# One encoder layer on one core: the first product of the feed-forward opening is moved ahead of four token blocks' transposes, and the first weights' low parts are moved to GpSimd

## The chip, the cores and the metric

One core of one Trainium2 chip runs the whole program. The metric is the device time of one execution in microseconds (us), the median of the runs shown. Engines: PE is TensorE's matmuls, PEld its weight loads, DVE is VectorE, ACT is ScalarE, POOL is GpSimd, SP is SyncE, which here only issues DMAs.

## What is computed

A prompt of 1024 tokens and a sample of 64 tokens, 1024 features each, go through one layer in float32:

```python
x = x + 0.5 * swiglu_1(rmsnorm(x, g_ffn1))   # w1_gate, w1_up: 1024 x 2816; w1_down: 2816 x 1024
x = x + mix(rmsnorm(x, g_mix))               # sliding-window attention and mLSTM heads
x = x + 0.5 * swiglu_2(rmsnorm(x, g_ffn2))
y = rmsnorm(x, g_final)
# rmsnorm(x, g) = x * rsqrt(mean(x * x) + 1e-6) * g;  swiglu(h) = (silu(h @ w_gate) * (h @ w_up)) @ w_down
```

The change lies in the opening of swiglu_1. The rest is as before, but for counts in waits that follow from it.

## The kernel before, in words

**Features on partitions.** The 1088 tokens come in nine blocks, eight of 128 and one of 64 (numbered 0 to 8). TensorE transposes each block in two halves of four tiles into PSUM banks (`start_transpose`, L836 to L846), ACT or DVE copies it from there to X (`start_evict_act`, L848; `start_evict_dve`, L853). The columns are worked on in two halves j of 544 tokens, and each of these in two pieces of 272 (n is 0 to 3 over all of them).

**Norm.** ACT squares and sums each block as it lies by tokens (`start_block_square`, L858) and takes the roots of a group of blocks (`start_block_root`, L866). DVE takes their reciprocals and writes them on diagonals (`start_diagonals`, L871). TensorE multiplies the diagonals by ones, which puts the scale of every token on all partitions in PSUM bank 4 + n (`start_roots`, L879). DVE scales a piece of X by it and by the gain (`start_scale`, L922).

**Split operands.** Every float32 operand is split in a high part, a copy to the matmul type on ACT (`start_high` L941, `start_weight_high` L957), and a low part, the difference of the two (`start_low` L948, `start_weight_low` L963, both on DVE). `three_pass` (L289) does three matmuls for one product of two split tiles.

**The first pair.** FFN columns come in pairs of 128. The first pair is multiplied out in 16 chains of 24 matmuls (`start_chain`, L967): four for the gate weights and four for the up weights (mat 0 and 1) in each half j. Chains of j 0 are worked on in pieces th of 272 tokens and column blocks fh. Chain i adds up in bank i. `start_silu` (L993, ACT) empties the gate banks, `start_gate` (L997, DVE) multiplies the up banks in. Later pairs use seven products instead of eight (`pe_stage`), which need differences of X's pieces: `start_difference` (L1004, DVE), `start_third_high` (L1024, ACT) and `start_third_low` (L1037, DVE) make them.

**X is scaled in place in the half j 1.** So SyncE first stores X to memory, in four DMAs xsp<-X (`spill`, L457 to L465): two for j 0, then two for j 1, which wait for ten copies by ACT (`x_evA`), that is for the last block. `start_scale` of j 1 waits for these stores (`x_out`, L932). SyncE's queue holds behind them the loads of the second pair's weights (RAWG, RAWU).

**Order.** Each engine's order is written out by hand: `start_pe_tokens` and `start_pe_pair` (L1045, L1053), `start_act_tokens` and `start_act_pair` (L1072, L1125), `start_dve_tokens` and `start_dve_pair` (L1136, L1191). GpSimd makes constants, issues small loads, and then has nothing to do until it adds weights for the second pair (`weight_sums`, L545 on). After the first pair `up_pe` runs the second pair's four stages (mat and j 0 or 1, seven products each). DVE empties their banks (L703), ACT copies some (L617), and both make the next weights' parts in between (L578, L583).

## Time and profile before

| | |
|---|---|
| median of 3 runs (lowest, highest) | 1945.61 us (1944.47, 1946.06) |
| the profiled execution's own time | 1945.54 us |
| its span in the profile | 1944.0 us |
| PE busy | 1924.2 us, 99% of the span |
| DVE, ACT, POOL busy | 1284.3, 783.4, 1053.3 us |
| mean granted TensorE clock | 0.998 of full speed |

Times in the rows are from the span's start. In a row of a timeline the columns are start, length, engine, line, operation, output and inputs, shapes and count. Rows of one kind that follow each other are merged, and "<-" in brackets names what ended the idle time ahead. A length can run into the next start, as the instructions of an engine overlap; the distance from start to start is what one of them takes of its engine.

### The profile page before, as it was taken

To read this page: it belongs to the slowest core of one execution; us is meant where nothing else is said; L and a number is where in the kernel's file an instruction comes from. 1 tells how busy PE (TensorE), PEld (TensorE's weight loads), DVE (VectorE), ACT (ScalarE), POOL (GpSimd) and SP (SyncE) were. 2 spreads that over 40 slices of the span, in tenths; PEclk is the share of its full clock that TensorE was granted. 3 is DMA by queue.
4 is the path that set the end of the run, shared out by engine and by line. 5 is a ranking of instruction groups with operands and counts; after the bars stand their busy time and mean duration, and the time that the engine had idled before them with its cause. 6 is when DMAs were issued, how large, how long until landed. Compare 5 with 4: busy or idle time off the path is not lost.

```text
span 1944.0 us, 39225 instructions
## 1 busy us (share of the span) xinstructions
PE 1924.2 (99%) x14627; PEld 1882.3 (97%) x14627; DVE 1284.3 (66%) x1882; ACT 783.4 (40%) x1595; POOL 1053.3 (54%) x958
## 2 busy tenths in 40 slices
PE   8999999999999999999999999999999999999998
PEld 7999999999999999999998999999999999999997
DVE  6866777666566788864445664866767667656674
ACT  6433333333443345733334542443333333344343
POOL 2277776775777641321222442237767776686770
PEclk9999999999999999999999999999999999999999
DMA  8135445334986530342332834214454444498552
GB/s 271 46 114 178 140 162 179 132 132 156 316 311 188 169 102 14 116 119 90 100 104 62 207 94 124 79 56 145 150 180 144 132 154 164 151 362 276 165 157 104
DMA packets 226846, 293.88 MB, mean 151 GB/s; under 512 B 16616, under 2 KB 158472, under 8 KB 226736
## 3 DMA queue, kind: packets, MB, share of 16 engines
q1 hardware_dynamic: 219040, 272.76, 43.8%
q0 software_dynamic: 7696, 19.63, 3.2%
q8 instruction: 71, 1.16, 0.3%
q14 instruction: 39, 0.32, 0.1%
HBM read 198.07 MB, written 94.21 MB: 150 GB/s over the span
## 4 chain that ended last, share of the span: by engine, by line
PE 96%; DVE 1%; DMA 1%; issue 1%; POOL 1%; ACT 0%; SPq 0%; ACTq 0%; POOLq 0%
PE bank L291 29%; PE bank L292 29%; PE bank L293 29%; PE bank L2583 1%; PE bank L2602 1%; PE bank L2593 1%; DMA XIN<-in_x_prompt 1%; PE bank L2514 0%; PE bank L1332 0%; PE bank L1334 0%; PE bank L1333 0%; PE bank L1328 0%; PE bank L845 0%; PE bank L2694 0%; PE bank L2692 0%
## 5 line engine op out<-in xcount | busy, mean ns | idle before, releaser
L291 PE MATMUL bank<-HA,HW 128*128 128x272 f32 x1120 | 322.7, 288 | 0.0
L292 PE MATMUL bank<-HA,HW 128*128 128x272 f32 x1120 | 322.3, 288 | 0.0
L293 PE MATMUL bank<-HA,HW 128*128 128x272 f32 x1120 | 322.1, 288 | 0.0
L1381 DVE SCALAR_TENSOR_TENSOR HW<-WRAW,HW 128x512 fp32r<-128x512 f32 x140 | 224.5, 1644 | 103.8 <-ACT HW L1376 103.3
L1387 POOL TENSOR_TENSOR HA<-ARAW,HA 128x544 fp32r<-128x544 f32 x140 | 222.6, 1607 | 101.8 <-ACT HA L1375 101.6
L291 PE MATMUL bank<-HL,WGH 128*128 128x368 f32 (+2 forms) x784 | 255.6, 326 | 0.0
L293 PE MATMUL bank<-HH,WGL 128*128 128x368 f32 (+2 forms) x784 | 246.3, 314 | 1.1 <-issue 1.1
L292 PE MATMUL bank<-HH,WGH 128*128 128x368 f32 (+2 forms) x784 | 246.2, 314 | 0.0
L292 PE MATMUL bank<-FC,WR 128*128 128x272 f32 x768 | 222.1, 289 | 0.0
L291 PE MATMUL bank<-FC,WR 128*128 128x272 f32 x768 | 220.4, 287 | 0.6 <-DVE WR L583 0.5
L293 PE MATMUL bank<-FC,WR 128*128 128x272 f32 x768 | 220.1, 287 | 0.0
L292 PEld LDWEIGHTS bank<-HA,HW 128*128 128x128 f32 x1120 | 211.1, 189 | 0.0
L293 PEld LDWEIGHTS bank<-HA,HW 128*128 128x128 f32 x1120 | 211.1, 189 | 0.0
L291 PEld LDWEIGHTS bank<-HA,HW 128*128 128x128 f32 x1120 | 210.5, 188 | 0.2 <-POOL HA L1387 0.2
L814 POOL TENSOR_TENSOR SA<-SA,PV 128x272 f32<-128x272 f32 x160 | 140.4, 898 | 101.3 <-DVE PV L703 98.1
L583 DVE TENSOR_TENSOR WR<-RAWU,WR 128x512 fp32r<-128x512 f32 x100 | 99.3, 993 | 134.3 <-ACT WR L578 134.3
L1375 ACT ACTIVATE HA<-ARAW 128x544 fp32r<-128x544 f32 x140 | 91.6, 654 | 232.3 <-PE bank L293 163.5
L629 ACT ACTIVATE SA<-SA 128x272 f32<-128x272 f32 x160 | 67.5, 431 | 265.9 <-POOL SA L768 137.0
L703 DVE TENSOR_TENSOR PV<-bank,PV 128x272 f32<-128x272 f32 x280 | 118.5, 435 | 77.6 <-POOL PV L765 38.5
L291 PEld LDWEIGHTS bank<-HL,WGH 128*128 128x128 f32 x784 | 147.3, 188 | 14.6 <-issue 12.9
L292 PEld LDWEIGHTS bank<-HH,WGH 128*128 128x128 f32 x784 | 147.5, 188 | 1.6
L293 PEld LDWEIGHTS bank<-HH,WGL 128*128 128x128 f32 x784 | 147.4, 188 | 1.0 <-issue 1.0
(384 smaller groups left out, 5670.6 us busy)
## 6 DMA issues: line engine op xcount, KB each, us to landing
asp<-SA SPq DMA_DIRECT2D x44, 544.0 KB, 3.5
RAWG<-in_w_gate SPq DMA_DIRECT2D x22, 1024.0 KB, 6.5
RAWU<-in_w_up SPq DMA_DIRECT2D x22, 1024.0 KB, 6.4
tsp<-TT SPq DMA_DIRECT2D x40, 544.0 KB, 6.6
ARAW<-tsp SPq DMA_DIRECT2D x80, 272.0 KB, 3.4
WS<-in_w_down SPq DMA_DIRECT2D x20, 1024.0 KB, 8.6
wsp<-WS SPq DMA_DIRECT2D x20, 1024.0 KB, 8.6
WRAW<-wsp SPq DMA_DIRECT2D x80, 256.0 KB, 4.3
```

Source lines behind the costliest of these rows:

```text
L291: nc.tensor.matmul(bank[:, 0:w], w_hi, rhs_lo, start=first, stop=False)
L292: nc.tensor.matmul(bank[:, 0:w], w_hi, rhs_hi, start=False, stop=False)
L293: return nc.tensor.matmul(bank[:, 0:w], w_lo, rhs_hi, start=False, stop=last)
L583: nc.vector.tensor_tensor(WR[:, o, 1], weight(o, q0, mat), WR[:, o, 0].bitcast(F32), ALU.subtract).then_inc(s_.lo, 1)
L629: nc.scalar.activation(tile, tile, ACT.Silu).then_inc(s_.silu, 1)
L703: nc.vector.tensor_tensor(out, bank, add, ALU.add).then_inc(s_.ev, 1)
L814: nc.gpsimd.tensor_tensor(gated(j, slot), gated(j, slot), PV[j][:, tile], ALU.mult).then_inc(s_.mul, 1)
L1375: nc.scalar.activation(HA[f][h][:, 0], ARAW[r][:, :, :], ACT.Copy).then_inc(down_hi, 1)
L1381: nc.vector.scalar_tensor_tensor(out=HW[f][h][:, 1], in0=WRAW[r][:, :], scalar=0.5, in1=HW[f][h][:, 0].bitcast(F32), op0=ALU.mult, op1=ALU ...
L1387: nc.gpsimd.tensor_tensor(HA[f][h][:, 1], ARAW[r][:, :, :], HA[f][h][:, 0].bitcast(F32), ALU.subtract).then_inc(down_alo, 1)
L2583: mm = nc.tensor.matmul(BANK[2 + i // 2][:, (i % 2) * 256:(i % 2) * 256 + 256], QB[rows, par, 2 * g_ + hl // 2, :], KW[rows, par, 0 if g_ ...
L2593: tr = nc.tensor.transpose(BANK[4 + w][:, i * P:(i + 1) * P], SP[:, i, w * P:(w + 1) * P], IDENT[:, :])
```

## The change

- TensorE: the first chain comes after block 4's transposes, ahead of blocks 5 to 8 and of the second scale row. Blocks 5 to 8 and the rows stand between the chains that follow. The third row stands inside the fifth chain, the fourth behind it.
- The first scale group of three blocks becomes two, of blocks 0 and 1 and of block 2.
- Block 3 is copied by DVE, and the second half of block 2 by ACT. Block 5 goes to banks 6 and 7, block 6 to banks 2 and 3, block 7 to banks 6 and 7.
- The eight low parts of the first weights are made by GpSimd instead of DVE. The first chain waits for one of them, and for the second in its middle.
- The 16 chains take banks 0 to 5 in turn instead of 0 to 3.
- ACT's order: first operands ahead of weights, all four up weights' high parts ahead of the squares of blocks 5, 6 and 7 and of block 8's copy.
- The j 1 stores wait for nine copies by ACT, which is block 8's again.

The diff, without hunks that only renumber counts:

```diff
         NORM_BANK = (4, 5, 4)
+        GROUP = ((0, 2, P), (2, 3, P), (3, 5, P), (5, 8, P), (8, 9, DEC))
+        ROOTS = len(GROUP)
...
             elif j:
-                sp.wait_ge(x_evA, 10)
+                sp.wait_ge(x_evA, 9)
             else:
-                sp.wait_ge(x_evV, 8)
-                sp.wait_ge(x_evA, 4)
+                sp.wait_ge(x_evV, 9)
+                sp.wait_ge(x_evA, 1)
...
-        BLOCK_BANK = (0, 2, 4, 6, 2, 0, 6, 2, 6)
-        ON_ACT = (3, 5, 6, 7, 8)
-        ON_DVE = (0, 1, 2, 4)
+        BLOCK_BANK = (0, 2, 4, 6, 2, 6, 2, 6, 6)
...
             pe.wait_ge(block_in[b], 16)
-            if b in (4, 5, 7):
-                pe.wait_ge(x_evV, {4: 4, 5: 2, 7: 8}[b])
-            elif b in (6, 8):
-                pe.wait_ge(x_evA, {6: 4, 8: 6}[b])
+            if b in (4, 5, 6):
+                pe.wait_ge(x_evV, {4: 4, 5: 7, 6: 9}[b])
+            elif b in (7, 8):
+                pe.wait_ge(x_evA, {7: 3, 8: 7}[b])
...
-        def start_evict_act(act, b):
-            for half in range(2):
+        def start_evict_act(act, b, halves=(0, 1)):
+            for half in halves:
...
-        def start_evict_dve(dve, b):
-            for half in range(2):
+        def start_evict_dve(dve, b, halves=(0, 1)):
+            for half in halves:
...
             pe.wait_ge(st.dg, (3, 5, 7, 9)[n])
             if n == 0:
-                pe.wait_ge(x_evV, 6)
-            elif n == 2:
-                pe.wait_ge(x_evA, 10)
+                pe.wait_ge(x_evV, 5)
+            elif n == 1:
+                pe.wait_ge(x_evA, 1)
+            else:
+                pe.wait_ge(x_evA, 9)
...
-                dve.wait_ge(x_evV, 6 if n == 0 else 8)
-                wait_done(dve, x_evA, (0, 4, 6, 10)[n])
+                dve.wait_ge(x_evV, 9 if n else 5)
+                wait_done(dve, x_evA, (kh, 1, 5, 9)[n])
...
+        def start_weight_low_pool(pool, i):
+            pool.wait_ge(st.whi, i + 1)
+            nc.gpsimd.tensor_tensor(WR[:, i, 1], first_weight(i), WR[:, i, 0].bitcast(F32), ALU.subtract).then_inc(st.wlo, 1)
...
+        def start_bank(f, mat, j, i):
+            return BANK[i if f else (8 * j + 4 * mat + i) % 6]
+
+        def start_bank_free(pe, mat, j, i):
+
+            q = 8 * j + 4 * mat + i
+            if q < 2:
+                pe.wait_ge(x_evV, 2)
+            elif q < 4:
+                pe.wait_ge(x_evA, 5)
+            elif q < 6:
+                pe.wait_ge(st.ht, 2 * i + 2)
+            elif q in (10, 11, 12, 13):
+                pe.wait_ge(st.mul, q - 9)
+            else:
+                pe.wait_ge(st.silu, {6: 1, 7: 2, 8: 3, 9: 4, 14: 5, 15: 6}[q])
+
         def start_chain(pe, f, mat, j, i, between=None):
             fh, th = (i // 2, i % 2) if mat and j else (i % 2, i // 2)
             if j == 0:
-                pe.wait_ge(st.wlo, 8 * f + 4 * mat + 2 * fh + 2)
-            if mat:
+                pe.wait_ge(st.wlo, 8 * f + 4 * mat + 2 * fh + (2 if f else 1))
+            if f == 0:
+                start_bank_free(pe, mat, j, i)
+            elif mat:
                 pe.wait_ge(st.silu, 8 * f + 4 * j + i + 1)
             elif j:
                 pe.wait_ge(st.mul, 8 * f + i + 1)
-            elif f:
+            else:
                 pe.wait_ge(o_add, OUT_STEPS - 4 + i + 1)
-            elif i < 2:
-                pe.wait_ge(x_evA, 2)
-            else:
-                pe.wait_ge(x_evA, 8)
             for kh in range(2):
                 e = 2 * th + kh
+                if f == 0 and j == 0 and kh:
+                    pe.wait_ge(st.wlo, 4 * mat + 2 * fh + 2)
...
-                    mm = three_pass(BANK[i], HT, WR[:, slot, 0, k], WR[:, slot, 1, k], product(PLACE[e], j, 0, k, f), product(PLACE[e], j, 1, k, f),
+                    mm = three_pass(start_bank(f, mat, j, i), HT, WR[:, slot, 0, k], WR[:, slot, 1, k], product(PLACE[e], j, 0, k, f), product(PLACE[e], j, 1, k, f),
...
-            nc.scalar.activation(gated(j, i % 2 * 2 + i // 2), BANK[i][:, 0:HT], ACT.Silu).then_inc(st.silu, 1)
+            nc.scalar.activation(gated(j, i % 2 * 2 + i // 2), start_bank(f, 0, j, i)[:, 0:HT], ACT.Silu).then_inc(st.silu, 1)
...
-            nc.vector.tensor_tensor(gated(j, slot), gated(j, slot), BANK[i][:, 0:HT], ALU.mult).then_inc(st.mul, 1)
+            nc.vector.tensor_tensor(gated(j, slot), gated(j, slot), start_bank(f, 1, j, i)[:, 0:HT], ALU.mult).then_inc(st.mul, 1)
...
         def start_pe_tokens(pe):
-            for b in range(3):
-                start_transpose(pe, b)
+            pe.wait_ge(const_ops, 7)
+            start_transpose(pe, 0)
+            start_transpose(pe, 1)
+            start_transpose(pe, 2)
             start_roots(pe, 0)
-            for b in range(3, 6):
-                start_transpose(pe, b)
-            start_roots(pe, 1)
+            start_transpose(pe, 3)
+            start_transpose(pe, 4)
 
         def start_pe_pair(pe, f):
             if f:
@@ -1058,47 +1080,51 @@
                         start_sum(pe, 3)
             else:
                 start_chain(pe, f, 0, 0, 0)
+                start_transpose(pe, 5)
+                start_roots(pe, 1)
                 start_transpose(pe, 6)
+                start_chain(pe, f, 0, 0, 1)
                 start_transpose(pe, 7)
-                start_chain(pe, f, 0, 0, 1)
+                start_chain(pe, f, 0, 0, 2)
                 start_transpose(pe, 8)
-                start_chain(pe, f, 0, 0, 2)
-                start_chain(pe, f, 0, 0, 3, between=lambda: start_roots(pe, 2))
+                start_chain(pe, f, 0, 0, 3)
+                start_chain(pe, f, 1, 0, 0, between=lambda: start_roots(pe, 2))
                 start_roots(pe, 3)
-            for mat, j in ((1, 0), (0, 1), (1, 1)):
+                for i in range(1, 4):
+                    start_chain(pe, f, 1, 0, i)
+            for mat, j in ((1, 0), (0, 1), (1, 1)) if f else ((0, 1), (1, 1)):
                 for i in range(4):
                     start_chain(pe, f, mat, j, i)
 
         def start_act_tokens(act):
-            for b in range(3):
-                start_block_square(act, b)
+            start_block_square(act, 0)
+            start_block_square(act, 1)
             start_block_root(act, 0)
+            start_block_square(act, 2)
+            start_block_root(act, 1)
+            start_evict_act(act, 2, (1,))
+            start_high(act, 0, 0, 0)
             start_weight_high(act, 0, 0)
+            start_high(act, 0, 0, 1)
             start_weight_high(act, 0, 1)
             start_block_square(act, 3)
-            start_high(act, 0, 0, 0)
             start_block_square(act, 4)
-            start_block_root(act, 1)
-            start_high(act, 0, 0, 1)
-            start_evict_act(act, 5)
-            start_evict_act(act, 3)
+            start_block_root(act, 2)
             start_weight_high(act, 0, 2)
             start_weight_high(act, 0, 3)
-            start_block_square(act, 5)
+            start_evict_act(act, 5)
             start_evict_act(act, 6)
             start_high(act, 0, 0, 2)
+            start_high(act, 0, 0, 3)
             start_evict_act(act, 7)
-            start_high(act, 0, 0, 3)
-            start_weight_high(act, 0, 4)
-            start_weight_high(act, 0, 5)
-            start_block_square(act, 6)
-            start_block_square(act, 7)
-            start_block_root(act, 2)
+            for i in range(4, 8):
+                start_weight_high(act, 0, i)
+            for b in (5, 6, 7):
+                start_block_square(act, b)
+            start_block_root(act, 3)
             start_evict_act(act, 8)
             start_block_square(act, 8)
-            start_block_root(act, 3)
-            start_weight_high(act, 0, 6)
-            start_weight_high(act, 0, 7)
+            start_block_root(act, 4)
...
         def start_dve_tokens(dve):
-            for b in range(3):
-                start_evict_dve(dve, b)
+            start_evict_dve(dve, 0)
+            start_evict_dve(dve, 1)
             start_diagonals(dve, 0)
+            start_evict_dve(dve, 2, (0,))
+            start_diagonals(dve, 1)
             start_scale(dve, 0, 0, 0, 0)
             start_scale(dve, 0, 0, 1, 0)
             start_low(dve, 0, 0, 0)
-            start_diagonals(dve, 1)
-            start_weight_low(dve, 0, 0)
-            start_weight_low(dve, 0, 1)
             start_low(dve, 0, 0, 1)
+            start_evict_dve(dve, 3)
+            start_diagonals(dve, 2)
             start_evict_dve(dve, 4)
-            start_weight_low(dve, 0, 2)
-            start_weight_low(dve, 0, 3)
             start_scale(dve, 0, 0, 0, 1)
             start_scale(dve, 0, 0, 1, 1)
             start_low(dve, 0, 0, 2)
             start_low(dve, 0, 0, 3)
-            start_weight_low(dve, 0, 4)
-            start_weight_low(dve, 0, 5)
-            start_diagonals(dve, 2)
             start_diagonals(dve, 3)
+            start_diagonals(dve, 4)
...
-            start_weight_low(dve, 0, 6)
-            start_weight_low(dve, 0, 7)
...
+            for i in range(8):
+                start_weight_low_pool(pool, i)
             up_pool(pool, 0)
             down_pool(pool, 0)
```

## Rows read from the trace of the kernel before

**Rows 1.** The page: busy time of each engine, share and instructions:

```profile
PE 1924.2 (99%) x14627; PEld 1882.3 (97%) x14627; DVE 1284.3 (66%) x1882; ACT 783.4 (40%) x1595; POOL 1053.3 (54%) x958
```

**Rows 2.** What TensorE waited for in the whole span: total, times, longest (us):

```profile
PE bank L888 <- DVE DG L877: 1.7, 1, 1.7
...
PE bank L291 <- DVE WR L583: 0.5, 1, 0.5
```

**Rows 3.** Timeline of PE, 5 to 37 us:

```profile
14.61 5.38 PE L845 MATMUL bank<-IDENT,XIN 128*128 128x128 f32 x24 [1.65 <-DMA XIN<-in_x_prompt]
...
20.73 0.36 PE L291 MATMUL bank<-FC,WR 128*128 128x272 f32 x1
...
23.80 1.91 PE L845 MATMUL bank<-IDENT,XIN 128*128 128x128 f32 x16
25.47 0.37 PE L291 MATMUL bank<-FC,WR 128*128 128x272 f32 x1
...
36.95 0.38 PE L291 MATMUL bank<-FC,WR 128*128 128x272 f32 x1
```

**Rows 4.** By windows: PE, PEld, DVE, ACT, POOL busy, granted clock, DMA share, GB/s:

```profile
13.00:14.00 1.00, 0.00 (x0) 0.00 (x0) 0.93 (x3) 0.51 (x1) 0.00 (x0) 0.54 1.00 353
...
19.00:20.00 1.00, 1.00 (x7) 1.00 (x6) 1.00 (x3) 0.70 (x2) 0.00 (x0) 0.55 1.06 195
```

**Rows 5.** Timeline of ACT, 13 to 37 us:

```profile
13.49 1.15 ACT L961 ACTIVATE WR<-RAWG 128x512 fp32r<-128x512 f32 x2 [3.06 <-DMA RAWG<-in_w_gate]
...
15.64 1.10 ACT L946 ACTIVATE FC<-HJ 128x1088 fp32r<-128x1088 f32 x1
...
22.52 1.07 ACT L862 ACTIVATE JK<-XIN 128x1024 f32<-128x1024 f32 x1
...
26.41 1.09 ACT L851 ACTIVATE X<-bank 128x512 f32<-128x512 f32 x2
...
28.37 1.17 ACT L961 ACTIVATE WR<-RAWU 128x512 fp32r<-128x512 f32 x2
...
30.67 1.06 ACT L862 ACTIVATE JK<-XIN 128x1024 f32<-128x1024 f32 x1
...
31.85 0.30 ACT L869 ACTIVATE RMB<-SSB,GQOE 128x3 f32<-128x3 f32 x1
32.05 0.64 ACT L851 ACTIVATE X<-bank 128x256 f32<-128x256 f32 x2
...
36.40 1.27 ACT L995 ACTIVATE SA<-bank 128x272 f32<-128x272 f32 x4
```

**Rows 6.** Timeline of SP, the first j 1 store:

```profile
32.72 0.36 SPq L465 DMA_DIRECT2D xsp<-X  x1
```

**Rows 7.** Timeline of DVE, 16 to 99 us:

```profile
16.77 1.29 DVE L950 TENSOR_TENSOR FC<-HJ,FC 128x1088 fp32r<-128x1088 f32 x1 [0.34 <-ACT FC L946]
...
37.27 1.72 DVE L935 SCALAR_TENSOR_TENSOR X<-X,GC,bank 128x272 f32<-128x272 f32 x4 [1.37 <-DMA xsp<-X]
40.95 1.72 DVE L935 SCALAR_TENSOR_TENSOR X<-X,GC,bank 128x272 f32<-128x272 f32 x4 [1.96 <-DMA xsp<-X]
...
94.59 0.69 DVE L583 TENSOR_TENSOR WR<-RAWU,WR 128x512 fp32r<-128x512 f32 x1 [1.02 <-ACT WR L578]
...
98.30 0.78 DVE L583 TENSOR_TENSOR WR<-RAWU,WR 128x512 fp32r<-128x512 f32 x1 [2.67 <-ACT WR L578]
```

**Rows 8.** The chain that ended last, 75 to 102 us: start, length, engine and line:

```profile
76.07 0.44 DVE PV L703
...
100.45 1.40 DVE WR L583
...
101.89 0.39 PE bank L291
```

**Rows 9.** Timeline of POOL, two of the second pair's additions:

```profile
45.49 1.29 POOL L556 TENSOR_TENSOR SS<-RAWG 128x512 f32<-128x512 f32 x1 [32.82 <-DMA RAWG<-in_w_gate]
...
73.18 2.24 POOL L556 TENSOR_TENSOR SS<-RAWU 128x512 f32<-128x512 f32 x1 [6.17 <-PE bank L293]
```

More of the change, by code:

```diff
@@ L271, in build @@
         down_mm, MM_FROM = x_tr, 2 * (NB + 1)
-        down_cp, CP_FROM = x_evA, 10
-        down_ev, EV_FROM = x_evV, 8
+        down_cp, CP_FROM = x_evA, 9
+        down_ev, EV_FROM = x_evV, 9
         down_hi, HI_FROM = dist_abs, 1
@@ L325, in norm_sum @@
             if n == 2:
-                pe.wait_ge(st.rs, 4 + 1)
+                pe.wait_ge(st.rs, ROOTS + 1)
             for h in range(2):
@@ L347, in norm_reciprocal @@
         def norm_reciprocal(dve, n):
-            dve.wait_ge(st.rs, 4 + n + 1)
+            dve.wait_ge(st.rs, ROOTS + n + 1)
             nc.vector.reciprocal(square_row(n), square_row(n)).then_inc(st.rc, 1)
@@ L352, in norm_scale @@
             w = NTILE[n][1]
-            dve.wait_ge(st.rc, 4 + n + 1)
+            dve.wait_ge(st.rc, ROOTS + n + 1)
             if n:
@@ L917, in start_reciprocal @@
         def start_reciprocal(dve, n):
-            dve.wait_ge(st.rs, 7 + n + 1)
+            dve.wait_ge(st.rs, ROOTS + 3 + n + 1)
             nc.vector.reciprocal(scale_row(1, n), scale_row(1, n)).then_inc(st.rc, 1)
@@ L924, in start_scale @@
             if f:
-                dve.wait_ge(st.rc, 7 + n + 1)
+                dve.wait_ge(st.rc, ROOTS + 3 + n + 1)
             else:
@@ L2138, in _ @@
                 nc.scalar.activation(FS[0:L, b % 4, 2:3], FS[0:L, b % 4, 2:3], ACT.Sqrt, bias=EPSC[0:L, 0:1], scale=1.0 / D).then_inc(st.rs, 1)
-            act.wait_ge(st.rc, 11 + NB + 1)
+            act.wait_ge(st.rc, ROOTS + 7 + NB + 1)
             act.wait_ge(fin_gain, GAIN_FROM + 1)
@@ L2480, in _ @@
                 nc.vector.tensor_tensor(f[:, 2:3], f[:, 0:1], f[:, 1:2], ALU.add).then_inc(fin_sum, 1)
-                dve.wait_ge(st.rs, 11 + b + 1)
+                dve.wait_ge(st.rs, ROOTS + 7 + b + 1)
                 nc.vector.reciprocal(f[:, 3:4], f[:, 2:3]).then_inc(st.rc, 1)
-                dve.wait_ge(st.rc, 11 + b + 1)
+                dve.wait_ge(st.rc, ROOTS + 7 + b + 1)
                 if 4 <= b < NB:
@@ L2508, in head_sums @@
                 if LAST_SUM[i] is None:
-                    pe.wait_ge(st.rs, 4 + (2 if HEAD_BANK[i] == 5 else 3))
+                    pe.wait_ge(st.rs, ROOTS + (2 if HEAD_BANK[i] == 5 else 3))
                 else:
```

2 lines of the change are left out of this document (removed).

## Prediction, made before the change was run

> **What bounds the kernel now.** I read the page first: PE is busy for 1924.2 of 1944.0 us [rows 1]. So the change can win only where TensorE stands still or runs at half clock, and it loses where it makes TensorE wait. Next what TensorE waited for [rows 2]: 1.7 us for the diagonals, before 14.61 us, and 0.5 us once for a low part of a weight. Then the timelines. In the PE timeline block 3 starts when its DMA lands, at 14.61 after 1.65 us of waiting, and from there TensorE runs on: 24 transposes, the second scale row, the first chain at 20.73 [rows 3]. The clock rows show why that start is slow: the granted clock is 0.54 of full speed over the window from 13 to 14 us and 0.55 over that from 19 to 20 [rows 4]. It fell to 1.2 GHz at about 13.1, after TensorE had waited for the diagonals and for block 3, and rose to 2.4 GHz at about 19.9, after unbroken work from 14.61. A transpose takes 5.38/24 = 0.224 us in the slow stretch and (25.47 - 23.80)/16 = 0.104 us after it [rows 3].
>
> The last view is the chain of waits, and it decides here. At 76.07 it leaves TensorE for DVE, and comes back only at 101.89, when TensorE has stood still for 0.5 us for the low part that DVE finished at 100.45 + 1.40 = 101.85 [rows 8, 2]. Between the two DVE, ACT and GpSimd answer each other, several us behind TensorE. Before 76.07 DVE's timeline is full back to 40.95; in its short pauses it only waits for ACT's copies of its own results. At 40.95 it had waited 1.96 us, and at 37.27 1.37 us, for the stores of X's second half [rows 7]. The first of these stores is issued at 32.72 and the second right behind it [rows 6], just after ACT's copy of block 8, which ends at 32.05 + 0.64 = 32.69 [rows 5]. **So two paths lead to 101.89: TensorE's own, 0.5 us short, and block 8's copy, stores, DVE.** The second sets the end of this stretch.
>
> **TensorE's part.** Same matmuls, other order. Up to 14.61 the path is the DMA of block 3, which nothing here moves: SyncE's loads are as before, and the wait for the constants only moves into a function. From 14.61 TensorE was never idle until 20.6 and must not be in the new kernel. Blocks 3 and 4 take 16 x 0.224 = 3.6 us, to 18.2. The first chain can start then if its inputs are there. Before, the operand's first low part ended at 16.77 + 1.29 = 18.06, though ACT's copy for it had stood behind two weight copies and a square, from 13.49 to 15.64 [rows 7, 5]. Now the roots of blocks 0 and 1 are taken before block 2 is there, so only one diagonal is left behind block 2. Of TensorE's 1.7 us of waiting for the diagonals I take 1.0 as saved, and scaling starts about 1 us earlier, near 12.0. ACT copies the first operand at once, to 14.7, the first weight to about 15.3 (1.15/2 each), the second operand (1.10) to 16.3 and the second weight to 16.9. DVE's low parts of the operands (1.29 each) are done by 16.3 and 17.6, GpSimd's first two (1.29 each alone [rows 9]) by 16.6 and 18.2. So the chain starts at 18.2 instead of 20.73.
>
> That is no gain in itself. The chain costs 23.80 - 20.73 = 3.07 us at full clock [rows 3], but until 19.9 it runs at half, so its first 1.7 us do only 0.85 us of work and it ends near 22.1. Block 5 and the second scale row then follow at full clock. The same work in the same clock ends at the same time. What is won: the first chain's pause of 0.1 us for block 5's copy, and the pause ahead of the fifth chain. That one started at 36.95 because the first SiLU, which empties its bank, started at 36.40 and ended near 36.8 [rows 3, 5]; with bank 4 it doesn't wait, about 0.3 us. What is lost: two more restarts of a chain behind transposes, some 0.1 us in all. Net: TensorE 0.3 us earlier (my bounds: 0 and 0.6). Banks 0 and 1 for the seventh and eighth chains need SiLU 1 and 2, near 38.5, at 42; nothing waits there.
>
> **GpSimd's low parts.** I bound the price by 1.29 and 2.24 us, the same kind of work at 45.49 and at 73.18, where DVE was subtracting SBUF tensors beside it [rows 9]. DVE makes its two operand low parts just beside the first two. The long price puts the second at 19.8, and the chain's middle needs it at 20.5, so I cost both ends at nothing. The Trainium skill, GPSIMD Engine Reference, section Key points, says that GpSimd shares its SBUF interfaces with VectorE and contends with instructions that have two SBUF inputs. By that rule these first two go at the long price; the trace agrees (2.24 against 1.29). It leaves 0.7 us of room instead of 2.4. The six later parts lie beside scaling that reads PSUM, or beside an idle DVE. GpSimd's small loads are issued before 13 us. The six subtractions that DVE is rid of after the first two save it nothing on the path: it waits for the stores at 37.27 anyway.
>
> **ACT's part, where I see the price.** Follow ACT to block 8's copy. Before, it did block 5's square at 22.52, while it waited for TensorE. It reached the up weights at 28.37, and then did two weight copies, two squares, one root and block 8 [rows 5]. Now block 5's transposes stand behind the first chain, so ACT has nothing from about 20.5 to 22.6. TensorE: first chain to 22.1, block 5 to 22.9, scale row to 23.5, block 6 to 24.3, second chain to 27.4, block 7 to 28.2. ACT copies the second half of block 7 at 28.4 (two halves took 1.09 at 26.41) and reaches the up weights at 28.9, 0.5 us later than before. Then four weight copies instead of two, + 1.1 us (1.17 for two), and three squares instead of two, + 1.2 us (31.85 - 30.67 = 1.18). Root and copy are the same. Block 8's copy ends at 32.7 + 0.5 + 1.1 + 1.2 = 35.5, **2.8 us later**. Both stores of j 1 and the weight loads behind them in SyncE's queue go 2.8 us later, with nothing else in the DMA queues in either case. GpSimd's additions to those weights and ACT's copies of them are used only when the first pair ends, after 60 us, which covers them.
>
> DVE then gets the stores at about 40.1 and 43.8, and all that follows is 2.8 us later, up to the low part that TensorE waited for at 101.85, now 104.65. TensorE waits longer there, in all 0.5 + 0.3 + 2.8 = 3.6 us over four products, and from 101.89 + 2.8 on it runs as before. The chains of j 1 still get their inputs in time: the ninth chain at 48.5 needs an operand at about 46.7, and its middle one at 48.3 for 50.0. The second pair's third product may pause some tenths for a gate near 75, inside the 3.6 us.
>
> **Sum.** 1945.54 us of the profiled execution (span 1944.0) + 2.8 = 1948.3. The median 1945.61 is 0.07 us off that execution, which changes nothing. Bounds of the term: 1.8, a third less, if DVE's pauses or the turns between engines swallow some of it, and 3.6, if the slower GpSimd and a late second weight part hold the first chain by 0.9 us.
>
> **Rivals.**
> 1. *The DVE path has slack* that the chain of waits doesn't show, or the stores are made up for (they land faster behind an empty queue). Then only TensorE's order counts: 0.3 us earlier, and at best the 0.5 us wait gone: 1944.8 to 1945.4. Against it: two waits of DVE for these very stores [rows 7]. For it: "the chain" names the last releaser only, and at 76.07 TensorE and DVE were ready within 0.1 us of each other.
> 2. *Slower by more: TensorE's longer wait costs the clock.* Before, it waited once, 0.5 us. Now four products of one stage wait. The low parts of the fourth and fifth came at 95.3 and 99.1 [rows 7], and will at 98.1 and 101.9; TensorE wants the fifth 1.5 us after the fourth (half a chain, 3.07/2), at 99.6. It stands still for 2.3 us of 3.8, and again 1.2 us before the sixth. At 13.1 the clock fell after two pauses of 1.7 and 1.65 us around the few matmuls of the first scale row, and stayed low for 6.8 us [rows 2 to 4]. If it falls for half of that time or all of it, half of 3.4 to 6.8 us is lost: 1950.0 to 1951.7. The Trainium skill, TensorE: Matmul & The Clock Gate, section HAM oscillation, says that waits between bursts of matmuls can send the array back to the slow clock each time. By that rule this rival is likelier when the waits lump together. It makes the kernel slower by 0.2% from about 1.1 us of loss on top of my sum. A clock that rises late in the opening, because the first chain's inputs come late and break the run from 14.61, costs as much.
> 3. *The change doesn't do what it says:* the first chain starts no earlier than about 20.7, because GpSimd or ACT is late. Then block 5 and ACT's rest come 1 us or more later too, and the price is 3.7 to 4.7: about 1949.7.
>
> **The numbers.** Forecast 0.55, rival 1 0.22, rival 2 0.17, rival 3 0.04, something else faster 0.02. A measurement of this kernel can tell about 0.2% from no change, 3.9 us. The forecast and rival 1 lie within it, rival 2 nearly all outside, rival 3 half; faster by 3.9 us would need more idle time than TensorE has after 14.61. So faster 0.02, within 0.2% 0.79, slower 0.19. The range, from rival 1's better half to the near part of rival 2: 1944.8 to 1950.6.
>
> **What would show it.** Right: first chain at 18 to 18.5 with its first matmuls at about 0.25 us each; fifth chain near 35 and without a pause; block 8's copy on ACT ending at 35 to 36; j 1 stores issued right behind it; DVE waiting for them until about 40 and 43.8; TensorE waiting 3 to 4 us for WR's low parts between 93 and 105. Wrong: stores no later than at 33.5; DVE's last store wait before 42.5; TensorE's wait near 102 under 1 us; a granted clock of 0.5 after 100 us (rival 2).

## The result, and the profile after

The changed kernel takes **1951.41 us** (median of 7 runs, 1950.75 to 1953.97), the kernel before, run beside it, 1945.59 us (7 runs, 1943.76 to 1946.06). The ratio is 1.0035, with a 95% interval of 1.0026 to 1.0044: slower by 0.35%. The forecast was 1948.3, its range ended at 1950.6, and the sign that it held likeliest was no difference. The profiled execution took 1950.83 us, its span is 1949.3, which is 5.3 us more than before.

What TensorE waited for, in the whole span (total, times, longest), rows that answer to [rows 2]:

```profile
PE bank L291 <- DVE SA L1023: 4.1, 1, 4.1
...
PE bank L888 <- DVE DG L875: 1.1, 1, 1.1
```

The wait for the diagonals is 0.6 us shorter, as the change wants, but the one behind it, for block 3's data, is 0.6 us longer (2.29 instead of 1.65 us), so the saving is not kept. The wait for a weight's low part is gone. One wait of 4.1 us is new. DVE's L1023 is the gate, the multiplication that empties an up bank.

The timeline of PE, first chain, the wait, and what followed:

```profile
17.65 0.59 PE L291 MATMUL bank<-FC,WR 128*128 128x272 f32 x1
18.04 0.43 PE L292 MATMUL bank<-FC,WR 128*128 128x272 f32 x1
18.27 0.43 PE L293 MATMUL bank<-FC,WR 128*128 128x272 f32 x1
...
74.39 0.28 PE L291 MATMUL bank<-FBa,WR 128*128 128x272 f32 x1
...
80.11 0.36 PE L291 MATMUL bank<-FXa,WR 128*128 128x272 f32 x1 [4.07 <-DVE SA L1023]
...
81.28 0.43 PE L293 MATMUL bank<-FXa,WR 128*128 128x272 f32 x1
81.51 0.43 PE L291 MATMUL bank<-FXa,WR 128*128 128x272 f32 x1
...
84.45 0.30 PE L292 MATMUL bank<-FBa,WR 128*128 128x272 f32 x1
84.60 0.29 PE L293 MATMUL bank<-FBa,WR 128*128 128x272 f32 x1
84.72 0.29 PE L291 MATMUL bank<-FT,WR 128*128 128x272 f32 x1
...
107.13 0.28 PE L291 MATMUL bank<-FC,WR 128*128 128x272 f32 x1
```

The second, third and fifth product in the kernel before:

```profile
74.38 0.28 PE L291 MATMUL bank<-FBa,WR 128*128 128x272 f32 x1
...
75.87 0.28 PE L291 MATMUL bank<-FXa,WR 128*128 128x272 f32 x1
...
78.86 0.28 PE L291 MATMUL bank<-FT,WR 128*128 128x272 f32 x1
```

The first chain starts at 17.65 with its matmuls 0.23 us apart, 3.1 us earlier than before [rows 3]. At 80.11 TensorE resumes after standing still for 4.07 us; its matmuls are 0.13 us apart at first, and from about 81.1 to 84.5 they are 0.23 us apart. The products side by side give the whole account: the second starts at the same time (74.39 and 74.38), the third 4.24 us later, the fifth 5.86 us later, so that the slow stretch took 1.62. The last row is the product that waited at 101.89 before [rows 8]; here it doesn't wait and is 5.24 us later, which is the loss of the whole span but for 0.1. That the two agree so well is partly chance: what lies behind this product took 1840.8 to 1842.5 us in the profiles of all kernels here (1844.1 in experiment 8), though nothing in it was changed. So this start is a finer yardstick than the span. By windows, columns as in [rows 4]:

```profile
78.00:80.00 2.00, 0.00 (x0) 0.00 (x0) 2.00 (x3) 0.35 (x1) 0.47 (x1) 1.00 0.00 0
80.00:82.00 2.00, 1.89 (x12) 1.92 (x13) 2.00 (x4) 0.77 (x1) 0.00 (x0) 0.77 0.00 0
82.00:84.00 2.00, 2.00 (x10) 2.00 (x10) 1.97 (x4) 0.40 (x1) 0.00 (x0) 0.50 0.79 252
```

The granted clock is still whole while TensorE stands still, and falls to 1.2 GHz about a microsecond after it resumes. It stays there for some 3.4 us.

**From ACT to the wait.** ACT's four up weights and its copy of block 8, then SyncE's queue, answering to [rows 5] and [rows 6]:

```profile
28.73 2.19 ACT L961 ACTIVATE WR<-RAWU 128x512 fp32r<-128x512 f32 x4
...
34.68 0.64 ACT L851 ACTIVATE X<-bank 128x256 f32<-128x256 f32 x2
```

```profile
36.95 1.39 SPq L398 DMA_DIRECT2D RAWG<-in_w_gate  x1
38.38 1.47 SPq L398 DMA_DIRECT2D RAWU<-in_w_up  x1
```

Block 8's copy ends at 35.32 instead of 32.69, 2.63 us later. DVE's timeline after, answering to [rows 7], with the stretch ahead of the late gate:

```profile
40.09 1.72 DVE L935 SCALAR_TENSOR_TENSOR X<-X,GC,bank 128x272 f32<-128x272 f32 x4 [2.81 <-DMA xsp<-X]
44.63 1.78 DVE L935 SCALAR_TENSOR_TENSOR X<-X,GC,bank 128x272 f32<-128x272 f32 x4 [2.82 <-DMA xsp<-X]
...
47.88 2.05 DVE L950 TENSOR_TENSOR FBa<-X,FBa 128x1088 fp32r<-128x1088 f32 x1
...
73.82 2.03 DVE L1041 TENSOR_TENSOR TS<-X,TS 128x1088 f32<-128x1088 f32 x1
75.78 1.57 DVE L585 TENSOR_TENSOR WR<-RAWG,WR 128x512 fp32r<-128x512 f32 x1
77.28 2.34 DVE L1041 TENSOR_TENSOR TS<-X 128x1088 f32<-128x1088 f32 x1
79.55 0.42 DVE L1023 TENSOR_TENSOR SA<-SA,bank 128x272 f32<-128x272 f32 x1
...
105.08 1.39 DVE L585 TENSOR_TENSOR WR<-RAWU,WR 128x512 fp32r<-128x512 f32 x1 [1.02 <-ACT WR L580]
```

The same gate and what stood ahead of it, in the kernel before:

```profile
69.63 1.28 DVE L1020 TENSOR_TENSOR TS<-X,TS 128x1088 f32<-128x1088 f32 x1
70.83 0.68 DVE L583 TENSOR_TENSOR WR<-RAWG,WR 128x512 fp32r<-128x512 f32 x1
71.44 1.28 DVE L1020 TENSOR_TENSOR TS<-X 128x1088 f32<-128x1088 f32 x1
72.64 0.42 DVE L1002 TENSOR_TENSOR SA<-SA,bank 128x272 f32<-128x272 f32 x1
```

The last wait for a store ends 3.68 us later, the first of the three instructions starts 4.19 us later, the gate behind them 6.91 us later. The three take 2.03, 1.57 and 2.34 us instead of 1.28, 0.68 and 1.28: 2.7 us more. GpSimd's timeline says what lies beside them:

```profile
73.19 1.51 POOL L558 TENSOR_TENSOR SS<-RAWU 128x512 f32<-128x512 f32 x1 [1.99 <-PE bank L293]
74.78 2.02 POOL L560 TENSOR_TENSOR SS<-SS,RAWU 128x512 f32<-128x512 f32 x1
76.77 1.70 POOL L561 TENSOR_TENSOR RAWU<-RAWU 128x512 f32<-128x512 f32 x1
```

These three additions start when TensorE ends the first pair, at 73.19 after and at 73.18 before [rows 9]. They did not move, and DVE did. Before, the gate was done when they began; now DVE's three instructions lie beside them, and both engines are slowed.

### The profile page after: what moved, and what is told of

Read it like the earlier page. It is cut to its first block, busy times and chain, and to the rows that moved or that the text cites. A ratio compares the mean times of both kernels' runs of the same rounds, so it can differ in the third digit from the quotient of the medians.

```text
span 1949.3 us, 39234 instructions
## 1 busy us (share of the span) xinstructions
PE 1926.6 (99%) x14627; PEld 1884.0 (97%) x14627; DVE 1280.5 (66%) x1876; ACT 783.2 (40%) x1595; POOL 1061.4 (54%) x966
## 4 chain that ended last, share of the span: by engine, by line
PE 96%; DVE 1%; POOL 1%; DMA 1%; issue 0%; ACT 0%; SPq 0%; ACTq 0%; POOLq 0%; DVEq 0%
PE bank L291 29%; PE bank L292 29%; PE bank L293 29%; PE bank L2605 1%; PE bank L2624 1%; PE bank L2615 1%; DMA XIN<-in_x_prompt 1%; PE bank L2536 0%; PE bank L1353 0%; PE bank L1354 0%; PE bank L1355 0%; PE bank L1349 0%; PE bank L2716 0%; PE bank L2714 0%; PE bank L2706 0%
```

## The experiments

All of them ran on the chip beside the kernel before, whose median was 1944.50 us on the chip of experiments 1 to 4, 1943.79 for 5 to 8, and 1944.34 for 9 to 11. The table gives the ratio to it with its interval, and from the profiled execution the end of the low part that set 101.85 before (DVE) and the start of the product that reads it (TensorE). Where the second is later than the first by more than 0.06 us, TensorE did not wait for the low part, and its own path set the start. As the kernel before itself took 1943.8 to 1945.6 us in the four sets of runs, a band given in us is loose by that much, and the ratios are what compares.

| | ratio [95%] | low part ends | product starts |
|---|---|---|---|
| before | 1 | 101.85 | 101.89 |
| after | 1.0035 [1.0026, 1.0044] | 106.47 | 107.13 |
| 1 copy of block 8 early | 1.0003 [0.9993, 1.0012] | 101.33 | 101.39 |
| 2 before, stores late | 1.0025 [1.0015, 1.0035] | 106.96 | 107.02 |
| 3 gates first | 1.0026 [1.0017, 1.0036] | 105.80 | 105.85 |
| 4 additions behind gates | 1.0025 [1.0014, 1.0035] | 105.51 | 105.56 |
| 5 loads behind stores | 1.0039 [1.0025, 1.0052] | 106.98 | 107.64 |
| 6 both, on after | 1.0008 [0.9999, 1.0017] | 102.06 | 102.11 |
| 7 both, on before | 0.9996 [0.9987, 1.0005] | 100.91 | 100.98 |
| 8 24 added matmuls | 1.0036 [1.0025, 1.0047] | 106.88 | 106.94 |
| 9 ACT's order alone, on after | 1.0007 [0.9998, 1.0016] | 100.79 | 100.84 |
| 10 copy early, on before | 1.0001 [0.9992, 1.0010] | 101.27 | 101.36 |
| 11 32 added matmuls | 1.0033 [1.0021, 1.0045] | 106.99 | 107.04 |

**1. Block 8's copy early, all else of the change kept.**

```diff
-            for b in (5, 6, 7):
+            start_block_square(act, 5)
+            start_evict_act(act, 8)
+            for b in (6, 7):
                 start_block_square(act, b)
             start_block_root(act, 3)
-            start_evict_act(act, 8)
```

> The changed kernel, but ACT copies block 8 behind the square of block 5, ahead of those of blocks 6 and 7. Theory A (ACT copies block 8 2.6 us later, so the j 1 stores and with them DVE's whole path are late): the copy ends near 32.7 us again, the first store is issued near 32.7, DVE waits for the last store until about 41, TensorE waits for no gate near 76, its clock stays up, and the time is that of the kernel before less up to 0.8 us: 1944.8 to 1945.8. Theory B (GpSimd's weight parts and the additions beside DVE are the cause, the stores are not): TensorE still waits 3 us or more near 76, and the time stays above 1949.5. Theory C (the first chain at half clock is the cause): above 1949.5 too, with no long wait later on.

Measured: 1944.68 us, ratio 1.0003, 0.1 us under the band that I gave, on a chip whose kernel before is itself 1.1 us faster. One moved call takes back 0.32 of the 0.35%. ACT and DVE of this kernel:

```profile
31.55 0.65 ACT L851 ACTIVATE X<-bank 128x256 f32<-128x256 f32 x2
```

```profile
74.66 0.43 DVE L1023 TENSOR_TENSOR SA<-SA,bank 128x272 f32<-128x272 f32 x1
```

Block 8 is copied by 32.20, the stores go out at 32.23, and the last gate is at 74.66. TensorE has no wait between 60 and 100 us, its clock stays whole there, and only the old wait is left (0.65 us, for the low part). So the copy's place on ACT is the root of nearly all of the loss; the opening's new order, with its low parts on GpSimd, is not. It is not quite free, though: here and in experiment 3, where the clock rose about 2 us earlier in the opening, TensorE waited 0.28 and 0.25 us for GpSimd's second low part at 19.73.

**2. The other way round: before, with the stores made late.** SyncE also waits for the eight low parts of the first weights.

```diff
             elif j:
                 sp.wait_ge(x_evA, 10)
+                sp.wait_ge(st.wlo, 8)
```

> The kernel before, with one wait more: SyncE issues the two j 1 stores only when the last low part of the first weights is done, near 35.9 us instead of 32.7. Nothing of the opening's order is changed. Theory A: DVE gets the last store near 44.5 instead of 41, TensorE waits 3 to 5 us, at a gate near 76 or spread over low parts near 100, and the time is 1949 to 1952. Theories B and C: within 0.7 us of the kernel before, 1945.0 to 1946.3.

Measured: 1949.24 us, ratio 1.0025, in the band of theory A. The stores go out at 35.57, and TensorE's waits from 70 us on are

```profile
78.97 0.36 PE L291 MATMUL bank<-FXa,WR 128*128 128x272 f32 x1 [0.62 <-DVE SA L1003]
82.16 0.37 PE L291 MATMUL bank<-FBa,WR 128*128 128x272 f32 x1 [1.46 <-DVE SA L1003]
...
107.02 0.39 PE L291 MATMUL bank<-FC,WR 128*128 128x272 f32 x1 [0.72 <-DVE WR L584]
```

Late stores alone, in the old kernel, cost most of what the change costs: the product starts at 107.02, 5.1 us late. Here the waits come in more pieces with matmuls between, and the granted clock stays whole. Two of them lie in the first pair already (0.46 us at 62.33 and 0.55 at 66.13, both for SiLU, which empties one of the four banks that the old order shares), so that the second pair's second product starts at 76.70, 2.3 us late. The changed kernel, with six banks, has none of these. 2.9 us of lateness at the store's issue became 4.17 us at DVE's second wait (45.12 against 40.95).

**3. Gates ahead of the differences and low parts.** The queue behind DVE's slow instructions is reordered, in the first pair only: gates 2 and 3 follow gate 1.

```diff
             start_gate(dve, f, 1, 1)
+            if not f:
+                start_gate(dve, f, 1, 2)
+                start_gate(dve, f, 1, 3)
             start_difference(dve, f, 1, 1)
             weight_low(dve, f, 1, 0, 3, first=True)
             start_difference(dve, f, 1, 2)
-            start_gate(dve, f, 1, 2)
+            if f:
+                start_gate(dve, f, 1, 2)
...
-            start_gate(dve, f, 1, 3)
+            if f:
+                start_gate(dve, f, 1, 3)
```

> The changed kernel, but in the first FFN DVE takes the last two gates of the first pair right behind the second of that half, ahead of two differences and a weight's low part. Theory A in its full form (DVE's path up to the low parts near 105 us sets the end): the wait at the third product near 76 goes, and TensorE waits instead for low parts of weights between 94 and 106, in all 4.5 to 5.5 us: 1949.8 to 1951.0, or 1.7 more if the clock falls there. If the price was only the gate's wait and the fall of the clock behind it: below 1947.

Measured: 1949.26 us, ratio 1.0026, which is 0.5 us under the band that I gave. The gate's wait and the clock's fall are both gone. In their place TensorE waits for low parts:

```profile
80.33 0.39 PE L291 MATMUL bank<-FT,WR 128*128 128x272 f32 x1 [1.12 <-DVE WR L585]
...
103.10 0.39 PE L291 MATMUL bank<-FT,WR 128*128 128x272 f32 x1 [1.58 <-DVE WR L585]
105.85 0.39 PE L291 MATMUL bank<-FC,WR 128*128 128x272 f32 x1 [0.97 <-DVE WR L585]
```

That is 3.7 us in three waits, less than the 4.5 to 5.5 that I expected, and the first of them lies earlier. It is near the 3.6 us of the first forecast, but by luck: that one came from a DVE 2.8 us late, and here DVE is 3.95 us late (105.80 against 101.85). The lag of DVE has to be paid once, and the order of DVE's instructions chooses where.

**4. GpSimd's additions behind the gates.**

```diff
             if first and mat:
                 pool.wait_ge(st.pm, 16 * f + 16)
+                if not f:
+                    pool.wait_ge(st.mul, 8)
```

> The changed kernel, but in the first FFN GpSimd starts the additions to the second pair's up weights only when the last gate of the first pair is done, so they no longer lie beside DVE's differences between 73 and 78 us. Expected from the contention seen in the trace: DVE's two differences and one low part there take 1.28, 1.28 and 0.69 us instead of 2.03, 2.34 and 1.57 (overlapped), so the gate comes 2.5 us earlier, TensorE waits about 1.5 us for it instead of 4.1, and its clock does not fall. Theory A: DVE is still 4 us late behind that, so the rest comes back as waits for low parts near 100: 1949.3 to 1950.8. If contention and clock were all of the price: about 1947.

Measured: 1949.38 us, ratio 1.0025, as theory A had it. DVE's three instructions, now alone, and the gate:

```profile
73.73 1.28 DVE L1043 TENSOR_TENSOR TS<-X,TS 128x1088 f32<-128x1088 f32 x1
74.93 0.68 DVE L587 TENSOR_TENSOR WR<-RAWG,WR 128x512 fp32r<-128x512 f32 x1
75.53 1.28 DVE L1043 TENSOR_TENSOR TS<-X 128x1088 f32<-128x1088 f32 x1
76.73 0.43 DVE L1025 TENSOR_TENSOR SA<-SA,bank 128x272 f32<-128x272 f32 x1
```

They are back to the durations of before, the gate comes at 76.73 instead of 79.55, TensorE waits 1.03 us for it instead of 4.07, and its clock stays whole. This shows that GpSimd beside DVE is what made this wait long. It also shows how little of it reaches the end: of the 2.8 us at the gate the low part gets 0.96 (105.51 instead of 106.47). The additions now slow what stands behind the gate, as they did in the kernel before, and DVE waits for ACT several times in between.

**5. The weight loads behind the landed stores.** I thought that SyncE's loads made the second store land late.

```diff
             sp.wait_ge(st.wlo, 8 * f + 4)
+            if not f:
+                for kh in range(2):
+                    sp.wait_ge(x_out[1][kh], 16)
             load_matrix(sp, f, 1, 0, w_gate)
```

> The changed kernel, but SyncE issues the loads of the second pair's weights only when both j 1 stores have landed. In the changed kernel the last store was late by 3.7 us at DVE though it was issued only 2.6 us late; both weight loads (1 MB each) were in the queues beside it. Theory A: the stores, issued near 35.3, land alone, the last near 42 instead of 44.6, DVE's path is 2.5 us earlier, TensorE waits under 2 us in all near 76 and under 2 us near 105, and the time is that of the kernel before plus 1 to 2.5: 1945.6 to 1947.2. If landing isn't shared with the loads, the last store stays near 44 and the time at 1950 or more.

A miss: 1951.58 us, ratio 1.0039. The stores go out at 35.33 and DVE goes on at 44.35, 9.0 us later, against 9.3 with the loads beside them. This kernel's DMA view from 42.0 to 44.3 us (40 slices, busy tenths and GB/s) shows that the wait for the second store goes on with no loads in the queues:

```profile
DMA  0000000000002000200020000000000000000000
GB/s 0 0 0 0 0 0 0 0 0 0 0 0 38 0 0 0 38 0 0 0 38 0 0 0 38 38 38 0 38 0 0 0 0 0 0 0 0 0 0 0
DMA packets 9, 0.02 MB, mean 7 GB/s; under 512 B 2, under 2 KB 2, under 8 KB 9
```

Nearly all of the data was out by 42, and DVE waited on through a tail of single packets and then silence. What that tail is I could not settle. The loads came 7 us later and moved GpSimd's first addition from 47.49 to 50.66 us, so that two low parts of DVE lay beside the additions instead of one, and nothing was gained; the wait of 4.09 us and the clock's fall were there again.

**6 and 7. The copy early and the loads behind the stores, on after and on before.** On after, block 5's square also goes into ACT's pause ahead of block 5's copy (1.52 us there). Beside the edit of experiment 5, on after:

```diff
+            start_block_square(act, 5)
             start_evict_act(act, 5)
...
-            for b in (5, 6, 7):
-                start_block_square(act, b)
-            start_block_root(act, 3)
+            start_block_square(act, 6)
             start_evict_act(act, 8)
+            start_block_square(act, 7)
+            start_block_root(act, 3)
```

On before:

```diff
+            start_evict_act(act, 8)
             start_block_square(act, 6)
             start_block_square(act, 7)
             start_block_root(act, 2)
-            start_evict_act(act, 8)
```

> The changed kernel with three edits that the theory points to: block 5's square goes into ACT's pause ahead of block 5's copy, block 8's copy behind the square of block 6, and the loads of the second pair's weights behind the landing of the j 1 stores. Theory A: stores issued near 32.5, last one landed near 39, DVE early enough that TensorE waits for nothing between 20 and 110 us. Then the opening's own gain (0.3 to 0.5 us) and the kernel before's wait of 0.5 to 0.7 us at a low part are both won: 0.6 to 1.2 us below the kernel before of the same chip, 0.9994 to 0.9997 of it. If DVE's path isn't what binds, the same as e1, 1.0000.

> The kernel before with the two edits on the stores alone: ACT copies block 8 ahead of the squares of blocks 6 and 7, and the loads of the second pair's weights wait until the j 1 stores have landed. The opening's order, banks and engines are as before. Theory A: stores issued near 30, last one landed near 36.5, the wait of 0.5 to 0.7 us near 101.9 goes, and the time is 0.4 to 0.8 us below the kernel before, 0.9996 to 0.9998. Against it: no change.

Measured: 1945.75 us (1.0008) and 1943.43 us (0.9996). The sixth missed: a wait of 0.99 us for the low part at 102.11 stayed, since GpSimd's additions slowed two of DVE's low parts near 50 us to 1.80 and 2.02 us. Its second store landed 7.8 us after the first one's issue, 0.5 sooner than with the loads beside it (8.3 in experiments 1 and 9), so the loads do slow the stores a little; but held back they put the additions beside DVE, which costs more. In the seventh DVE did not wait for the stores at all and TensorE did not wait at 101. Its ratio is at the lower end of the band, but its interval still holds 1.

**8 and 11. What the clock's fall costs.** TensorE gets 24, then 32, more matmuls ahead of the third product's waits, into a bank that nothing uses; their results are thrown away. The edit of 8, with a range of 8 in 11:

```diff
             for o in range(PRODUCTS):
+                if first and f == 0 and mat == 0 and j == 0 and o == 2:
+                    for fill in range(6):
+                        for k in range(4):
+                            nc.tensor.matmul(BANK[7][:, 0:HT], WR[:, 0, 0, k], product(0, j, 0, k, f), start=True, stop=True)
```

> The changed kernel with 24 more matmuls on TensorE, into a bank that nothing reads, ahead of the wait for the gate near 76 us; their results are not used. They take 3.0 us of the 4.1 us that TensorE stood still there. Theory: the fall of the clock behind that wait (from about 81 to 84.5 us in the trace of the changed kernel, 1.7 us of work lost) is a cost of its own; with TensorE busy the clock stays at 2.4 GHz, the wait behind them is about 1 us, and the time drops by 0.8 to 1.7 us to 1949.2 to 1950.2, where DVE's own path (4.6 us late near 105) ends it. If the clock's fall costs nothing beyond DVE's lateness: unchanged, 1950.7 to 1951.5.

> After, with 32 matmuls more (not 24) ahead of the waits of the second pair's third product, into a bank that nothing uses, their results thrown away; they take 32 x 0.131 = 4.2 us, as long as TensorE stood still there, 4.07 us. My theory (the pause costs its length and 1.7 us of slow clock on top): the clock stays up after 81 us, the wait there is under 0.3 us, and the runs whose mean clock is 0.998 or more lie at 1948.0 to 1949.8, 1.5 to 3 us under the kernel after the change, though TensorE has 32 matmuls more to do. Rival (the fall of the clock is no part of the loss, or the added matmuls cost what they save): the same runs lie at 1950.5 to 1952.

Measured: 1950.22 us (1.0036) and 1949.91 us (1.0033), against 1.0035 for the changed kernel. By the ratio the eighth gained nothing and missed, though 1950.22 is only just above its band: its chip's kernel before is 1.8 us faster. In it TensorE waits 1.10 us behind the added matmuls, as expected. The eleventh's timeline:

```profile
76.60 4.14 PE L597 MATMUL bank<-FC,WR 128*128 128x272 f32 x32
80.66 0.36 PE L291 MATMUL bank<-FXa,WR 128*128 128x272 f32 x1
80.86 0.29 PE L292 MATMUL bank<-FXa,WR 128*128 128x272 f32 x1
...
107.04 0.39 PE L291 MATMUL bank<-FC,WR 128*128 128x272 f32 x1 [0.69 <-DVE WR L585]
```

The gap is filled, the clock is whole in the profiles of both from 76 to 110 us, and the matmuls behind it are 0.12 us apart. Yet the product starts at 107.04, only 0.09 us earlier than in the changed kernel. This small difference says little by itself, since in this execution the clock rose 1.4 us later in the opening and the stores went out 1.1 us later (36.45); what says more is what the product waited for. Of the eleventh's four runs with a mean clock of 0.998 two lie in the band that I gave (1949.10 and 1949.50) and two above it (1950.32 and 1950.56). What I had left out is the table's other column. With the clock whole TensorE is early, and waits 0.69 us for a low part that DVE ends at 106.99. The fall takes 1.6 us on TensorE's path, but that path was behind DVE's by only 0.66 us (107.13 against 106.47). So in the changed kernel's profile its net price is at most those 0.66 us, too little for the medians to show.

**9 and 10. ACT's order alone, on after and on before**, without experiment 5's edit. On after:

```diff
+            start_block_square(act, 5)
             start_evict_act(act, 5)
...
-            for b in (5, 6, 7):
+            start_evict_act(act, 8)
+            for b in (6, 7):
                 start_block_square(act, b)
             start_block_root(act, 3)
-            start_evict_act(act, 8)
```

> After, with ScalarE's order alone mended: block 5's square goes into the pause ahead of block 5's copy, and block 8's copy stands ahead of the squares of blocks 6 and 7; SyncE is left alone. My theory: the stores are issued near 32 us, as in the run with the early copy, GpSimd's additions start with the end of the first pair and not later, so that DVE's low parts near 48 to 52 us take 1.28 us and not 1.8 to 2.0, TensorE waits under 0.8 us near 101, its clock stays up, and the ratio is 0.998 to 1.000 (median 0.9993). Rival (the loads behind the stores did no harm, what was left of the loss lies in the opening itself): ratio 1.0005 to 1.0015, with a wait of about 1 us at 102.

> Before, with block 8's copy alone moved ahead of the squares of blocks 6 and 7; SyncE is left alone. My theory: this edit does all that the pair of edits did: the stores are issued near 30 us, DVE does not wait for them, the 0.5 us wait for a low part near 102 us goes, and the span is 1941.5 to 1943, ratio 0.9990 to 0.9998. Rival (the moved loads did it): stores near 30, but DVE waits for them still or TensorE still waits 0.3 us or more near 102, ratio 0.9998 to 1.0003.

Measured: 1945.39 us (1.0007) and 1943.94 us (1.0001). In the ninth the trace is as my theory had it (stores at 31.78, low parts of 1.28 to 1.40 us near 50, a wait of 0.43 us near 101, the product at 100.84), and the ratio is as the rival had it. Its profiled execution, with a span of 1941.8, was the fastest of its 11 runs. In the tenth DVE still waited 0.95 us for a store, the wait near 102 was gone, and the ratio is the rival's.

No version here can be told from the kernel before as faster. The new opening order may even cost something with the copy in its place. Experiments 6 and 7 ran on one chip and differ by 2.3 us (the lowest of the sixth's 11 runs, 1944.54, is above ten of the seventh's 11), experiments 9 and 10 by 1.4 us, which is less sure; each time the new order is the slower. In both pairs its copy of block 8 still ends later (32.2 against 29.8 us, and 31.8 against 30.2), so it is not shown what makes this rest of about 0.1%.

## Why the prediction was wrong

By its own steps:

- **TensorE's part: right but for the 0.3 us.** The first chain started at 17.65, a little earlier than the 18.2 forecast, and at half clock. Of the 1.0 us to be saved at the diagonals 0.6 came, and the wait for block 3's data took it back. Of the 0.3 us that TensorE was to be earlier nothing is left at 74.39; that the clock rose at 19.9 in one profile and 19.6 in the other weighs as much. The fifth chain had its bank: TensorE waited for none.
- **GpSimd's first low parts: right.** They cost nothing on the path here, as costed, though the first two took 2.07 us each. In experiments 1 and 3 the second held TensorE for 0.3 us. What the forecast left out shows here already: DVE's operand low part beside them took 2.12 us (at 16.62), not 1.29.
- **ACT's part: right.** Forecast 2.8 us late, measured 2.63. Experiments 1 and 2 show from both sides that this is the cause of most of the loss.
- **"DVE then gets the stores at about 40.1 and 43.8, and all that follows is 2.8 us later": the first step that failed.** The first was 40.09, the second 44.63. The second store took 9.3 us from the first one's issue instead of 8.2, which made 3.7 us of 2.6. A low part of DVE slowed by GpSimd (2.05 instead of 1.28 us at 47.88, where in the kernel before another one took 1.62 at 48.95) made 4.2 of it. I had moved a wait's end as if a DMA's landing and all durations behind it were fixed.
- **"The second pair's third product may pause some tenths for a gate near 75": the step that gave the wrong place and size.** It paused for 4.07 us. I had the row of GpSimd's additions at 73.18 and 2.24 us, and knew that they start with the end of the first pair. I didn't ask what of DVE's would now lie beside them. Experiment 4 takes 2.8 us off that gate by moving them alone.
- **"TensorE waits 3.6 us over four products near 93 to 105": not seen in the changed kernel**, since the pause at 76 had already used up TensorE's lead. In experiment 3, where the gate goes first, 3.7 us of such waits come back.
- **Rival 2 had the event, but not its place or price.** A long wait did cost the clock, 3.4 us at half speed, at 81 and not at 98 to 102. Its time, 1950.0 to 1951.7, holds the measured 1951.41, but by luck: it put 1.7 to 3.4 us on the clock and 2.8 on DVE, and the runs show at most 0.66 net for the clock and 4.6 for DVE. The Trainium skill, TensorE: Matmul & The Clock Gate, section HAM oscillation, tells of a kernel whose waits between bursts sent the array back to the slow clock each time; the trace agrees for the one wait of 4.07 us. Waits of 0.6 to 1.6 us in experiments 2 to 4 left the clock whole.
- **Rivals 1 and 3 did not come.** DVE's path had no slack for the stores (experiment 2), and the first chain started at 17.65, not near 20.7.

**The sum as it came out.** On TensorE's path, up to the product at 107.13: 0.0 for the opening, + 4.24 for the gate (the wait of 4.07 and the restart), + 1.62 for the clock, and - 0.62 for the old wait of 0.5 and its restart: 5.24 us. On DVE's path, up to the low part's end: + 2.63 for the copy, + 1.05 for the store's landing, + 0.5 beside GpSimd at 47.88, and the 0.45 that is left of what the gate's three instructions lost, since before GpSimd slowed the ones behind them: 4.63 us. The forecast's term was this second sum, taken as 2.8. Mis-sized by 1.8 us, it alone would have ended at about 1950.2 (1945.54 + 4.63); the remaining 0.6 us is the gate and the clock. This accounts for the profiled execution, 1950.83 us; why the median of the seven runs is another 0.6 us above it, no trace here shows. The two paths lie close, so removing one cause alone (experiments 3, 4, 8, 11) gives back 1.6 us in the product's start, or less. Only the cause they share gives back 5.7 (experiment 1: 101.39).

What stays open: why the second store lands 9.2 to 9.6 us after the first one's issue when this is at 35.0 to 36.5 us, and 8.2 to 8.4 us after it when it is at 30.2 to 32.7, with the loads behind it in either case. Without them it is 9.0 (experiment 5) and 7.8 (experiment 6), so the gap is there too.

## What to carry to other kernels

Two short copies and a square more ahead of one copy, on an engine that is 40% busy, cost most of 0.35%, because a store, a slow engine and the bound engine hang on that copy in a row: before adding work to an idle engine's queue, follow the one instruction in it that releases a DMA. When a chain is shifted, don't add the shift to its end; lay the shifted chain beside everything that does not shift, as the work of an engine that shares its memory, and price the pairs that newly overlap. And compute the end of every path to the next joint: where two are within a microsecond, what one of them loses or gains is mostly hidden by the other.

## What the runs showed of the hardware

- DVE's subtractions of two SBUF tensors took 1.28 us alone and up to 2.4 us beside GpSimd's additions and subtractions (2.0 to 2.4 in the changed kernel), the 0.68 us ones up to 1.57. GpSimd's took 1.29 us alone and 1.4 to 2.4 beside DVE's. Both lose at once, which the forecast had for GpSimd only. The Trainium skill, GPSIMD Engine Reference, section Key points, names this contention; the trace agrees and gives it the size.
- The clock stayed whole during a wait of 4.07 us and fell a microsecond after work had resumed. It also fell in experiment 8's profiled execution at about 1157 us, in a stage of small matmuls where no other profile here shows it. That was nearly 7 us at half clock, from which I estimate a cost of some 3 us. It may be behind runs like its 1953.66, of which there is no trace. A row of that profile:

```profile
1158.00:1160.00 2.00, 2.00 (x10) 2.00 (x10) 1.92 (x8) 0.07 (x1) 0.00 (x0) 0.50 0.00 0
```

- In the opening the clock rose at between 17.5 and 21.1 us in single executions of the changed kernel and its variants, whose instructions up to there are the same (17.1 in experiment 2, 19.9 in the kernel before). Block 8's copy ended at 35.0 to 36.4 us in the six kernels with one order of ACT. So a difference of less than about 1.4 us between two single profiles proves little; that between the product's start and the low part's end, within one profile, can be read.
